# Last four slabs of each output stage used tile by tile, in a two-layer decoder trunk on one core

## The reference, cut to what matters

```python
for l in range(DEPTH):                      # 2 layers, x is (512 tokens, 1024 columns) in fp32
    ...                                     # three mixers and sigmoid gates give `merged`
    x = layer_norm(DEEPNORM_ALPHA * x + merged @ w_out[l], ln_g[l, 0], ln_b[l, 0])
    h_gate, h_up = jnp.split(x @ ffn_w_in[l], 2, axis=-1)          # 2 x 2816 columns
    x = layer_norm(DEEPNORM_ALPHA * x + (jax.nn.silu(h_gate) * h_up) @ ffn_w_out[l], ln_g[l, 1], ln_b[l, 1])

def layer_norm(x, g, b):
    mu = jnp.mean(xf, -1, keepdims=True)
    var = jnp.mean(jnp.square(xf - mu), -1, keepdims=True)
    return ((xf - mu) * lax.rsqrt(var + LN_EPS) * g + b).astype(x.dtype)
```

## Time and profile before

| what | us |
|---|---|
| median of 3 runs (1780.27 to 1780.75) | 1780.42 |
| the profiled execution's own time | 1778.62 |
| its span, first to last instruction | 1776.8 |
| PE busy in the span | 1730.8 (97%) |
| DVE busy | 940.1 (53%) |
| ACT busy | 651.3 (37%) |
| granted TensorE clock, mean | 0.997 of full speed |

### The profile page before, as it was taken

How to read it: one execution, slowest core, us unless ns; L and a number is a source line. 1 busy time by engine, 2 the same in 40 slices (tenths; PEclk the granted TensorE clock), 3 DMA queues, 4 the chain that set the end, 5 groups by cost and what they waited for, 6 DMA issues and landing times.

```text
span 1776.8 us, 26563 instructions
## 1 busy us (share of the span) xinstructions
PE 1730.8 (97%) x10044; PEld 1406.8 (79%) x10044; DVE 940.1 (53%) x1522; ACT 651.3 (37%) x1152; POOL 125.3 (7%) x252
## 2 busy tenths in 40 slices
PE   7989999999999999999999999999999999999998
PEld 6767777788888888888887777777888888888886
DVE  5688777554454444422357977775453544444223
ACT  4334565522242232221353355654222522223213
POOL 4710000000000000000037000000000000000000
PEclk9999999999999999999999999999999999999999
DMA  7532111122523222222263421111333222222222
GB/s 258 165 97 76 57 56 48 53 103 95 168 72 106 95 94 94 94 95 95 89 246 109 102 80 54 54 49 59 107 107 125 77 95 98 101 96 94 95 95 83
DMA packets 65917, 174.86 MB, mean 98 GB/s; under 512 B 14256, under 2 KB 26576, under 8 KB 65056
## 3 DMA queue, kind: packets, MB, share of 16 engines
q1 hardware_dynamic: 40192, 140.53, 23.6%
q10 hardware_dynamic: 21888, 13.64, 3.1%
q0 software_dynamic: 3744, 19.41, 3.1%
HBM read 162.27 MB, written 7.08 MB: 95 GB/s over the span
## 4 chain that ended last, share of the span: by engine, by line
PE 88%; DVE 6%; DVEq 2%; ACT 2%; issue 1%; DMA 0%; ACTq 0%
PE ps L523 19%; PE ps L525 18%; PE ps L524 18%; PE ps L563 6%; PE ps L561 6%; PE ps L562 6%; PE ps L840 2%; PE ps L827 2%; PE ps L813 2%; DVE ta L1363 1%; PE ps L664 1%; PE ps L552 1%; PE ps L541 1%; DVE wlo L1357 1%; PE ps L816 1%
## 5 line engine op out<-in xcount | busy, mean ns | idle before, releaser
L523 PE MATMUL ps<-xh,whi 128*128 128x512 f32 x1312 | 520.2, 396 | 5.3 <-ACT gates L1173 2.1
L525 PE MATMUL ps<-xh,wlo 128*128 128x512 f32 x1312 | 512.2, 390 | 0.0
L524 PE MATMUL ps<-xl,whi 128*128 128x512 f32 x1312 | 511.5, 390 | 0.0
L1357 DVE TENSOR_TENSOR wlo<-raw,whi 128x1024 fp32r<-128x1024 f32 x264 | 324.7, 1230 | 342.0 <-ACT whi L961 331.7
L961 ACT ACTIVATE whi<-raw 128x1024 fp32r<-128x1024 f32 x264 | 278.6, 1055 | 350.7 <-PE ps L563 234.2
L523 PEld LDWEIGHTS ps<-xh,whi 128*128 128x128 f32 x1312 | 246.9, 188 | 59.5 <-DVE wlo L1357 3.6
L525 PEld LDWEIGHTS ps<-xh,wlo 128*128 128x128 f32 x1312 | 246.6, 188 | 52.7
L524 PEld LDWEIGHTS ps<-xl,whi 128*128 128x128 f32 x1312 | 247.1, 188 | 49.0
L561 PE MATMUL ps<-whi,hh 128*128 128x512 f32 x352 | 137.5, 391 | 0.0
L563 PE MATMUL ps<-whi,hl 128*128 128x512 f32 x352 | 137.0, 389 | 0.0
L562 PE MATMUL ps<-wlo,hh 128*128 128x512 f32 x352 | 137.0, 389 | 0.0
(11 more groups left out here) (335 smaller groups left out, 2325.4 us busy)
## 6 DMA issues: line engine op xcount, KB each, us to landing
raw<-wstream SPq DMA_DIRECT2D x264, 512.0 KB, 3.2
w<-w1s POOLq DMA_DIRECT2D x4, 2048.0 KB, 12.5
sm<-smalls POOLq DMA_DIRECT2D x2, 1060.0 KB, 6.6
xt<-xin ACTq DMA_DIRECT2D x4, 512.0 KB, 6.4
scratch_u<-pa ACTq DMA_DIRECT2D x8, 256.0 KB
toep<-scratch_k ACTq DMA_DIRECT2D x4, 512.0 KB
toep_b<-scratch_k ACTq DMA_DIRECT2D x4, 512.0 KB
xt<-xin POOLq DMA_DIRECT2D x4, 512.0 KB, 4.0
```

The source lines that it names most:

```text
L523: pe.matmul(ps[:, bank, :], wh, hi[:, k, :], start=first and i == 0, stop=False)
L524: pe.matmul(ps[:, bank, :], wh, lo[:, k, :], start=False, stop=False)
L525: m = pe.matmul(ps[:, bank, :], wl, hi[:, k, :], start=False, stop=last and i == len(blocks) - 1)
L1357: dve.tensor_tensor(wlo[:, c % 2, :], raw[:, c % 2, :], whi[:, c % 2, :].bitcast(f32), SUB).then_inc(lo_ready, 1)
```

## The change

Six things are changed, all in the four output stages and in what follows each.

1. Of each output stage's last six slabs the order in the weight stream is turned, so that what were the last two (E and F here) come ahead of the four others (A, B, C, D). E and F are split into buffers of their own (`end_hi`, `end_lo`, over memory that is free then), without waiting for the ring.
2. The last four slabs of fh = 1 (C and D in the ring, E and F in their own buffers) are used tile by tile: each tile gets all its 24 matmuls before the next. Tiles 0 to 2 take the order C, E, F, D, then half 0 is turned, and tile 3 takes C, D, E, F, freeing C and D early.
3. In `ln_part` ACT applies the gain of half 0 first and splits the next stage's two slabs behind it, one after the other. DVE does the four `halves` of half 0, then the two `split_lo`, and only then the statistics of tile 3. The statistics of fh = 0 come after the stage's last `split_lo`.
4. In `first_pair` the turning of half 1 comes after quarter 2 of slab 1, and in the second half of tokens the two slabs alternate quarter by quarter, so that slab 0 is freed one quarter before slab 1.
5. After n = 3 tiles 2 and 3 are normed each by itself, and turned each by itself (`turn_last`) into the banks that half 0 had.
6. Small arrays of the norm are placed elsewhere, and POOL's wait before it loads `w1` counts tiles instead of slabs.

```diff
 to_tokens, fh = 0 and 1, then the end of fh = 1
-                    for s in range(pairs - 2 * fh):
-                        c = at + fh * pairs + s
+                    for s in range(pairs - 4 * fh):
+                        i = fh * pairs + s
+                        c = at + i + (2 if i >= early else 0)
...
-                        m.then_inc(slab_done, 1)
+                        m.then_inc(slab_done, 3 if i == early - 1 else 1)
...
-                for t in (2, 3):
-                    m = token_products(a % 2, 1, t, k, hi, lo, False)
-                m.then_inc(slab_done, 1)
-                token_products(b % 2, 1, 2, k + 2, hi, lo, True).then_inc(t_psum, 1)
-                turn_back(n, 0, rt)
-                token_products(b % 2, 1, 3, k + 2, hi, lo, True).then_inc(slab_done, 1)
+                for t in range(4):
+                    order = (0, 1, 2, 3) if t == 3 else (0, 2, 3, 1)
+                    for i in order:
+                        if t == 0 and i < 2:
+                            pe.wait_ge(lo_ready, a + i + 3)
+                        m = token_products(*src[i], 1, t, 2 * (pairs - 4 + i), hi, lo, i == order[-1])
+                        if t == 3 and i < 2:
+                            m.then_inc(slab_done, 1)
+                    m.then_inc(t_psum, 1)
+                    if t == 2:
+                        turn_back(n, 0, rt)
 first_pair
-                if n:
-                    turn_back(n - 1, 1, rt)
                 pe.wait_ge(lo_ready, at + 4)
                 for g in range(4):
+                    if n and g == 3:
+                        turn_back(n - 1, 1, rt)
                     x_quarter(at + 1, 0, g, n * 8)
-                for c in range(2):
-                    for g in range(4):
+                for g in range(4):
+                    for c in range(2):
                         m = x_quarter(at + c, 1, g, n * 8)
-                    m.then_inc(slab_done, 1)
+                        if g == 3:
+                            m.then_inc(slab_done, 1)
 after n = 3
+            def turn_last(n, rt):
+
+                pe.wait_ge(ln_first, n + 2)
+                pe.wait_ge(ln_second, n * 4 + 3)
+                pe.wait_ge(ln_x, n * 8 + 2)
+                pe.wait_ge(x_ready, n * 8 + 10)
+                turn_tiles(n, 1, 0, (0,), rt)
+                pe.wait_ge(ln_first, n + 3)
+                pe.wait_ge(ln_second, n * 4 + 4)
+                turn_tiles(n, 1, 0, (1,), rt)
 ACT, splits of the output stage
+                k = at + c
+                act.wait_ge(raw_loaded[k % 2], (k // 2 + 1) * 16)
+                if e < 2:
+                    act.activation(end_hi[n % 2][e][:, :], raw[:, k % 2, :], ACT.Copy).then_inc(hi_ready, 1)
+                else:
+                    act.wait_ge(slab_done, k - 1)
+                    act.activation(whi[:, k % 2, :], raw[:, k % 2, :], ACT.Copy).then_inc(hi_ready, 1)
 packed, at the end of by_tokens
+            last = stream[l, n - 6:n]
+            last[:] = last[[4, 5, 0, 1, 2, 3]]
```

More of the change, by code:

```diff
@@ L240, in build_program @@
     tg2 = place("tg2", big_at + 20480, [P, 2, S])
[L242 to L245, removed]
+    gq_at = used["gq"][0]
+    lnst = place("lnst", gq_at, [P, 4, 2, 6])
+    lnmv = place("lnmv", gq_at + 48, [P, 4, 2])
+    lnrs = place("lnrs", gq_at + 56, [P, 4])
+    lnnb = place("lnnb", gq_at + 64, [P, 4])
+    end_hi, end_lo = [], []
+    for at in ([big_at + 16384 + 1024 * i for i in range(4)], [kv_at, kv_at + 1024, kv_at + 2048, ys_at + 3072]):
+        k = len(end_hi)
+        end_hi.append([place("end_hi%d%d" % (k, i), at[i], [P, 1024], f32r) for i in range(2)])
+        end_lo.append([place("end_lo%d%d" % (k, i), at[2 + i], [P, 1024], f32r) for i in range(2)])
     ft = place("ft", ys_at, [P, 2, S])
@@ L458, in _ @@
                 if l:
-                    wait(slab_done, l * NSLAB + 2)
+                    wait(t_psum, l * 8)
                     load_w1()
@@ L559, in token_products @@
                     a, b = hi[:, k0 + q, P * t:P * t + P], lo[:, k0 + q, P * t:P * t + P]
[L560 to L563, removed]
-                return m
[L566 to L570, removed]
+                    cols = slice(S * q, S * q + S)
@@ L571, in turn_back, with turn_tiles @@
+                    pe.matmul(dst, a, wh[:, cols], start=False, stop=False)
+                    pe.matmul(dst, a, wl[:, cols], start=False, stop=False)
+                    m = pe.matmul(dst, b, wh[:, cols], start=False, stop=last and q == 1)
+                return m
+            def turn_tiles(n, half, bank_half, ts, rt):
                 for g in range(4):
                     for m in range(2):
-                        for t in range(2):
-                            x = pe.transpose(ps[:, turned_bank(half, g), 2 * P * m + P * t:2 * P * m + P * t + P],
+                        for t in ts:
+                            x = pe.transpose(ps[:, turned_bank(bank_half, g), 2 * P * m + P * t:2 * P * m + P * t + P],
@@ L578, in to_tokens @@
             def to_tokens(n, at, pairs, hi, lo, freed, taken, each, rt):
+                early = 2 * pairs - 6
                 for fh in range(2):
@@ L961, in split_hi, with out_stage_split, deviations, normalized @@
                 act.activation(whi[:, c % 2, :], raw[:, c % 2, :], ACT.Copy).then_inc(hi_ready, 1)
+            def out_stage_split(n, at, c, pairs):
+                e = c - (2 * pairs - 6)
+                if e not in (0, 1, 2, 3):
+                    split_hi(0, at + c)
+                    return
+                k = at + c
[5 more added lines that the diff above has]
+                    act.activation(whi[:, k % 2, :], raw[:, k % 2, :], ACT.Copy).then_inc(hi_ready, 1)
             def slab_out(h, c):
                 act.wait_ge(slab_done, h * 2 + (c + 3))
-            def deviations(n, half):
-                pair = slice(2 * half, 2 * half + 2)
-                act.wait_ge(ln_var, n * 2 + half + 1)
+            def deviations(n, step, tiles):
+                pair = slice(tiles[0], tiles[-1] + 1)
+                act.wait_ge(ln_var, n * 2 + step + 1)
                 act.activation(lnrs[:, pair], lnrs[:, pair], ACT.Sqrt).then_inc(ln_sd, 1)
[L972 to L976, removed]
+            def normalized(n, step, tiles, rt):
+                act.wait_ge(ln_scalars, n * 2 + step + 1)
+                for t in tiles:
+                    for fh in (0, 1) if t > 1 and n < 2 * L - 1 else (1,):
                         x = act.activation(rt[:, t, S * fh:S * fh + S], ps[:, tile_bank(fh, t), :], ACT.Identity,
@@ L995, in ln_part @@
                 last = n == 2 * L - 1
[L996 to L999, removed]
+                deviations(n, 0, (0, 1))
+                normalized(n, 0, (0, 1), rt)
+                if last:
+                    deviations(n, 1, (2,))
+                    normalized(n, 1, (2,), rt)
                 for g in range(4):
                     gained(n, 0, g, rt, last)
-                deviations(n, 1)
-                if not last:
+                if last:
+                    deviations(n, 2, (3,))
+                    normalized(n, 2, (3,), rt)
+                else:
+                    split_hi(0, next_slab)
                     split_hi(0, next_slab + 1)
-                normalized(n, 1, rt)
+                    deviations(n, 1, (2, 3))
+                    normalized(n, 1, (2, 3), rt)
                 for g in range(4):
@@ L1426, in second_stats, with variances, scalars @@
                 dve.bn_aggr(lnmv[:, t, :], lnst[:, t, :, :].rearrange("p f s -> p (f s)"))
-            def variances(half):
-                pair = slice(2 * half, 2 * half + 2)
+            def variances(tiles):
+                pair = slice(tiles[0], tiles[-1] + 1)
                 dve.drain()
                 dve.tensor_scalar(lnrs[:, pair], lnmv[:, pair, 1], EPS / ALPHA ** 2, None, ADD).then_inc(ln_var, 1)
-            def scalars(n, half):
-                pair = slice(2 * half, 2 * half + 2)
-                dve.wait_ge(ln_sd, n * 2 + half + 1)
+            def scalars(n, step, tiles):
+                pair = slice(tiles[0], tiles[-1] + 1)
+                dve.wait_ge(ln_sd, n * 2 + step + 1)
                 dve.reciprocal(lnrs[:, pair], lnrs[:, pair])
@@ L1459, in ln_part, with first_columns @@
             def ln_part(n, next_slab, rt):
-                def first_columns(half):
-                    for t in (2 * half, 2 * half + 1):
+                def first_columns(tiles):
+                    for t in tiles:
                         x = dve.tensor_scalar(rt[:, t, 0:S], ps[:, tile_bank(0, t), :], lnmv[:, t, 0:1], lnrs[:, t:t + 1], SUB, MUL)
@@ L1467, in ln_part @@
                 last = n == 2 * L - 1
[L1468 to L1473, removed]
+                second_stats(n, 0)
+                second_stats(n, 1)
+                variances((0, 1))
+                scalars(n, 0, (0, 1))
+                first_columns((0, 1))
+                second_stats(n, 2)
+                if last:
```

(14 more changed lines are left out.)

58 lines of the change are left out of this document (30 added, 28 removed).

## The result

The changed kernel takes 1788.61 us (median of 5 runs, 1786.54 to 1792.18) against 1780.32 for the kernel before in the same runs: a ratio of 1.0049, 95% interval 1.0037 to 1.0060. It is slower by 8.3 us. I had forecast 1782.2, range 1776.6 to 1785.6. Its runs also spread over 5.6 us where before's five spread over 0.9.

A forecast was written before the change was run, and what follows sets the result against it. PE, busy 97% of the span, was taken as the bound, so only waits and the end could move: 3 x 0.9 us lost at handovers less 0.9 at the end, +1.8 on 1780.42, gave 1782.2 us, range 1776.6 to 1785.6.

The forecast's parts named there:

- Slab 2's wait: Behind each handover's first pair, PE waits 2.3 us for slab 2's low part, since slab 0 is freed later.
- T3: End of tile 3's last matmul in an output stage (517.05 at n = 0), forecast to stay where it was.
- wait of A, C or D: Output stages: C and D no wait, A taken as 0; rival of A late at n = 0 and 2, 1785.4, chance 0.07.
- The waits of half 1: In each handover's first pair: new waits of 0.8 us before half 1's turning and 0.65 us for its x.
- The handovers: From tile 3's end to slab 2 at n = 0, 1, 2: a loss of 0.9 us each, +2.7 us together.
- The end: After n = 3, tile 3 turned alone and four stores back to back: -0.9 us, bounds -0.3 and -1.9.
- my sum of +1.8: Whole kernel: 3 x 0.9 lost at the handovers less 0.9 gained at the end, +1.8 us.
- A loss of 0.9 us for each handover, all three: Slab 2 starts at 534.4 against 533.5 at n = 0, repeated at n = 1 and 2: +2.7 us.
- The rival that came true: At slab 2 the clock falls to half speed in the new gap: 1783.9, 1785.6 or 1787.3 by falls; chance 0.2.
- My price for one: One clock fall at slab 2: 3.4 us of work at half speed lose 1.7 us.
- 1.25 us of each handover: First pair at each handover ends at 532.1 against 533.35, a gain of 1.25 us before slab 2's wait.

The follow-up runs named there:

- Experiment 3: The changed kernel, alternating the two slabs only in the first pair at the kernel's start, slab by slab at the three handovers: 1782.50 us, ratio 1.0018.
- experiment 5: The changed kernel with ten matmuls that nobody reads behind each first pair, where PE waits for slab 2: 1783.51 us, ratio 1.0015.
- experiment 2: The kernel before, with only the alternating order of the two slabs in the second half of tokens added: 1793.87 us, ratio 1.0086.
- experiment 1: The changed kernel, with the second half of tokens of each first pair slab by slab again: 1777.04 us, ratio 0.9983.
- Experiment 4: The changed kernel, with slab 0 freed two quarters before the first pair's end instead of one: 1779.20 us, ratio 0.9997.
- experiment 9: The changed kernel, alternating only in the start's first pair, with ten unread matmuls in the wait for slab 2 there: 1781.67 us, ratio 1.0009.

## Why the prediction was wrong

**What held.** Slab 2's wait: 2.33 us foreseen, 2.34 measured at each handover. T3 against the stage's start stayed (48.9 us from the first residual, both traces). No wait of A, C or D came up. The waits of half 1: 0.8 foreseen for the turning and 0.65 for x; the rows give 0.48 + 0.16 = 0.64 and 0.48. The handovers cost 0.66, 1.03 and 0.65, 2.3 us against the 2.7 of the sum. The end gained 0.9, as summed, and its four pieces of x ran back to back, at 338 to 343 GB/s. Of my sum of +1.8 these terms measured +1.4.

**The step that failed** is the count of places: "A loss of 0.9 us for each handover, all three". `first_pair` is called four times. At the kernel's start it has no norm ahead of it, so none of the gain, but it has the alternating order, and so the whole 2.2 us, which my sum had at nothing. I had looked only where an output stage ends. Experiment 3 prices the place at 5.5 us by the medians. The traces put 2.1 to 2.7 of that on the late slab itself; where the rest comes from they don't show. By its wait alone the fourth place would have moved the forecast to 1782.2 + 2.2 = 1784.4, still inside the range. What took the time out of it is that place together with the falls.

**The rival that came true** is the fall of the clock in the new gap, which I gave 0.2. Three falls stood behind the four gaps in the profiled run, 1.55 to 1.6 us each, and filling the gaps in experiment 5 gave 5.1 us. 1784.4 and 5.1 make 1789.5, against 1788.6 measured. My price for one was right (1.7). I forecast a gap of 2.3 us, longer than any that had kept the clock in before's trace (1.95 us), next to a stretch at 0.50 behind PE busy for 1.40 us of 3.4; those rows spoke for at least one fall in three gaps, not for one chance in five. They didn't speak for a fall at each: over the traces of the changed kernel and of experiments 2 and 3, four of nine unfilled gaps of 2.34 us had one behind them. TensorE: Matmul & The Clock Gate, section Why this matters for your kernels, of the Trainium skill warns of idle gaps between bursts of matmuls, but only of gaps longer than these. So it would not have given this answer, and the measurement decides.

**A gain that I put on the wrong account.** I took 1.25 us of each handover for the new norm and turning order, and expected it of experiment 1. Measured there are 0.36, -0.02 and 0.36. Most of it was the alternating order, through x. The part that costs is also the part that gives. Experiment 4 keeps the whole gain with the first two quarters alternating, so the last two give nothing and only cost.

What stays open is why the start's late slab costs 4.6 us with the filler in experiment 9, and where in the mixers the falls come; for that one trace of each kernel is too few.

## What to carry to other kernels

When an order is changed in a helper, count its calls first, the ones far from the stage that it was changed for too. In a ring of two buffers the last use of the older buffer sets when the next tile can start: interleave the early part of two tiles, where it hides a slow supply, and finish the older one first. And a new gap of 2 us on TensorE belongs in the range with the price of the half-speed stretch that can follow it, 1.6 us each here.

## What the runs showed of the hardware

Four of the nine unfilled gaps of 2.34 us in the traces had a stretch of 3.4 us at a granted clock of 0.50 (1.2 GHz) behind them: three of four in the changed kernel, one of four in experiment 2, none of one in experiment 3. PE had been busy for 1.2 to 1.3 us of the 3.4 ahead of each in the changed kernel, with a fall and without. None of the four gaps of 1.62 us in experiment 4 had one. A fall cost 1.55 to 1.6 us.

Products that nobody needs, put into the four gaps, made the kernel 5.1 us faster. Put into the one at the start alone they gave 0.8 us or less.

The spread of the runs can't be put down to the gaps. The changed kernel's five runs spread over 5.6 us (1786.5 to 1792.2) and before's first five over 0.9, but before's 25 runs beside the first experiments went from 1777.5 to 1782.6.
